# A two-model kernel whose expert weights stream from HBM: nine ring slots for eight, more expert chunks held aside and spread over the sequence, later gate-weighted selections, and a final norm on token-major rows

## The chip, the cores and the metric

One Trainium2 chip, one of its cores, one launch. The metric is the device time of the whole program in microseconds (us); lower is better. All data are float32.

## The reference, cut to what matters

The kernel runs two models one after the other on 256 tokens of 1024 features. The first has two layers (a stick-breaking attention and a dilated attention, each followed by a convolutional feed-forward net). The second has two layers (DEPTH = 2) on the 256 tokens and, in its first layer, on 256 context tokens too. Each layer modulates its input by a vector made from `c @ w_ada` (the "ada" panels), runs three branches (neighbourhood attention with a position bias, differential attention, a gated MLP), merges them, and ends in a mixture of 16 experts in which every expert picks its 32 best tokens:

```python
def ec_moe(h, w_r, w1, w3, w2):
    aff = jax.nn.softmax((h @ w_r).astype(jnp.float32), axis=-1)
    gate, idx = lax.top_k(jnp.swapaxes(aff, 1, 2), cap)          # cap = 32
    xin = jax.vmap(lambda hb, ib: hb[ib])(h, idx)
    hid = jax.nn.silu(jnp.einsum('becd,edf->becf', xin, w1)) * jnp.einsum('becd,edf->becf', xin, w3)
    ye = jnp.einsum('becf,efd->becd', hid, w2) * gate[..., None].astype(h.dtype)
    return jax.vmap(lambda yb, ib: jnp.zeros((n, D), h.dtype).at[ib.reshape(-1)].add(yb.reshape(-1, D)))(ye, idx)
```

After the last layer comes `rmsnorm(x, g_final)`. Each layer's experts have 16 x 3 matrices of 1024 x 1024, 201 MB, and each weight is used once.

## The kernel before

**Chunks.** `weight_chunks` (L196) lists all weights in the order in which TensorE needs them, cut into chunks of 1 MB (SLOT = 2048 words in each of 128 partitions). SyncE (`@block.sync`, L1205) walks the list and issues one DMA a chunk into a ring of NSLOT = 8 slots; before a chunk goes out it waits until the chunk eight places earlier has been used (L1225). TensorE waits for a chunk's semaphore and then reads it.

**Chunks held aside.** Some expert chunks don't go through the ring. `held` (L232) names them: places 8 to 15 of the expert chunks in layer 0 and places 8 to 17 in layer 1. They go to parts of SBUF that are free at the time (`held_slots`, L445), and SyncE issues them before the ring chunks named in `early`: the first 5 (7 in layer 1) once the attention is over, 3 more once the gates of the merge are done. So when the first expert starts, a stock of 8 + 8 chunks (8 + 10 in layer 1) can lie in SBUF.

**Experts** (L1149 to L1178). A layer has 192 expert chunks. Expert e takes 8 chunks for w1 and w3 (`expert_up`), then 4 for w2 of expert e-1 (`expert_down`), then a transpose of its hidden rows (`expert_turn`); the matmuls are at L1120. In layer 0 an expert has 64 rows (32 tokens and 32 of the context), in layer 1 it has 32, so that a chunk costs 8 matmuls of 512 columns in layer 0 and 16 of 256 in layer 1. Experts are handled in packs of four: `gather` (L1063, matmuls L1074) collects the tokens of a pack with a 0/1 selection matrix SEL, after e = 2, 6, 10 for the next pack; `scatter` (L1092, matmuls L1100) adds a finished pack back. `turn_gates` (L1078), after e = 1, transposes GSEL, the selection weighted by the gates, which VectorE makes (L1906) right after the first pack's copies and ahead of expert 0.

**Router.** After `w_out` TensorE makes the router's logits (L1033, L1041), VectorE and ScalarE turn them into affinities, TensorE transposes those (L1050), then does the ada panels of this place (`ada_gap`, 3 panels in layer 0 and 2 in layer 1: `ada_part`, L622, reads two chunks and frees their slots; `ada_fold`, L638, reads what ScalarE has copied from a part), and then waits for VectorE's top-k, which ends at L1860 (`pos_ready`), to transpose the places (L1059). VectorE builds SEL0 (L1883), and `gather(0)` starts.

**From layer 0 to layer 1.** After the last expert TensorE does two ada parts, `scatter(3)`, two folds; then the squares' mean (L553, L563), two more ada parts, and, once ScalarE has scaled and shifted the normed input (`scale_shift`, L2012), the first panel of w_in, two folds, the second panel.

**GpSimd's queue** issues the small loads. In each layer of the second model, once `dma_free` is set: lambda, norm and router rows, then the position bias, which is written to a scratch tensor, sheared from there into another one with 8 DMAs (L2334), and loaded as tiles with 16 DMAs (L2340). VectorE uses the tiles at L1658.

**The end.** `norm(X, S)` squares on ScalarE, sums on TensorE (L553, L563), VectorE multiplies (L1306), TensorE transposes 16 blocks (L1195), ScalarE copies, and SyncE stores the result with one DMA (L1227).

## Time and profile before

| | us |
|---|---|
| median of 3 runs (lowest to highest) | 2883.66 (2879.49 to 2886.35) |
| the profiled execution | 2883.96 |
| its span in the profile | 2882.2 |
| TensorE matmul busy | 2611.2 (91%) |
| VectorE busy | 810.2 (28%) |
| ScalarE busy | 449.5 (16%) |
| GpSimd busy | 55.4 (2%) |
| TensorE matmul, L1120 (experts) | 595.4 in 4384 instructions |
| chain that ended last: TensorE L506 (the feature-major projections) | 40% |
| chain that ended last: DMA of expert weights to the ring | 22% |

How to read it: the profile gives one execution, cut into busy time by engine and by source line; PE is TensorE, PEld its weight loads, DVE VectorE, ACT ScalarE, POOL GpSimd, SP SyncE. A "window" row gives what each engine did in a stretch, the granted TensorE clock, the busy share of the 16 DMA engines and what they moved. A timeline row gives start, duration, line, operation, what was written and read, the count, and in brackets how long the engine sat idle before and what released it. From these two the experts' stretches can be taken apart: layer 0's run from 1523 to 1993 us, layer 1's from 2415 to 2859 us.

### The profile page before, as it was taken

Reading aid. Unit: us, or ns where it says so; the run is one execution under the profiler, and the core shown is the slowest. Engines: PE = TensorE matmul, PEld = TensorE weight load, DVE = VectorE, ACT = ScalarE, POOL = GpSimd, SP = SyncE. Lnnn points to the kernel's source line nnn. Section 1 sums busy time; section 2 is a strip of 40 time slices with the busy share of each in tenths; the row PEclk is TensorE's granted clock in tenths of the full one; section 3 lists DMA queues with packets and bytes.
Section 4 is the critical chain, followed back from the end, with each engine's and each line's share of the span. In section 5 each row is a group of like instructions: output and inputs, shape, how many; then the busy total and the mean of one; then the engine's idle time right before and its main releaser. Section 6 shows DMA issues by size and latency. Waiting matters only on the chain.

```text
span 2882.2 us, 30967 instructions
## 1 busy us (share of the span) xinstructions
PE 2611.2 (91%) x13335; PEld 1547.2 (54%) x13335; DVE 810.2 (28%) x1764; ACT 449.5 (16%) x1002; POOL 55.4 (2%) x85
## 2 busy tenths in 40 slices
PE   8999999999999999999999898987999998666665
PEld 5678878578873445444444342332556885232322
DVE  2535511435512454332121121112344422010101
ACT  1320010230011022222021101112111311000001
POOL 1000000000003000000000000000200000000000
PEclk9999999999999999999999999999999999776877
DMA  8654444464456111121527999999721367999996
GB/s 276 222 162 149 173 161 146 163 217 146 169 173 168 67 59 59 44 73 59 204 105 324 420 421 421 421 421 386 178 88 67 124 262 322 421 421 421 420 421 259
DMA packets 201019, 663.81 MB, mean 230 GB/s; under 512 B 13426, under 2 KB 58784, under 8 KB 151732
## 3 DMA queue, kind: packets, MB, share of 16 engines
q1 hardware_dynamic: 192912, 641.97, 58.2%
q0 software_dynamic: 7776, 19.81, 3.1%
q8 instruction: 106, 1.74, 0.3%
q14 instruction: 29, 0.24, 0.0%
q10 hardware_dynamic: 196, 0.06, 0.0%
HBM read 660.67 MB, written 9.57 MB: 233 GB/s over the span
## 4 chain that ended last, share of the span: by engine, by line
PE 72%; DMA 23%; DVE 3%; ACT 2%; issue 1%; ACTq 0%; DVEq 0%
PE ps L506 40%; DMA ring<-in_w_e 22%; PE ps L527 8%; PE ps L1120 7%; PE ps L687 5%; PE ps L1074 1%; PE ps L622 1%; PE ps L1100 1%; PE ps L935 1%; PE ps L957 1%; PE ps L890 1%; PE ps L903 1%; DMA ring<-in_w_ada 1%; PE ps L878 1%; PE ps L553 1%
## 5 line engine op out<-in xcount | busy, mean ns | idle before, releaser
L506 PE MATMUL ps<-normed,ring 128*128 128x256 f32 (+1 forms) x3456 | 942.8, 433 | 12.4 <-ACT normed L2012 8.8
L506 PEld LDWEIGHTS ps<-normed,ring 128*128 128x128 f32 x3456 | 653.6, 191 | 279.3 <-issue 201.3
L1120 PE MATMUL ps<-ring,arena 128*32 128x256 f32 (+1 forms) x4384 | 595.4, 527 | 195.6 <-DMA ring<-in_w_e 187.3
L1120 PEld LDWEIGHTS ps<-ring,arena 128*32 128x32 f32 (+1 forms) x4384 | 194.9, 133 | 576.7 <-DMA ring<-in_w_e 286.8
L506 PE MATMUL ps<-arena,ring 128*128 128x256 f32 (+1 forms) x832 | 254.0, 462 | 1.3 <-DVE small L1248 1.3
L527 PE MATMUL ps<-ring,normed 128*128 128x512 f32 x512 | 222.8, 593 | 0.0
L506 PEld LDWEIGHTS ps<-arena,ring 128*128 128x128 f32 x832 | 156.1, 190 | 88.1 <-issue 73.1
L1329 DVE COPY arena<-ps 128x256 f32<-128x256 f32 (+1 forms) x102 | 55.9, 554 | 418.4 <-PE ps L506 173.1
L527 PEld LDWEIGHTS ps<-ring,normed 128*128 128x128 f32 x512 | 96.2, 190 | 116.2 <-issue 116.1
L687 PE MATMUL ps<-arena,ring 128*128 128x256 f32 x704 | 152.3, 379 | 0.0
L687 PEld LDWEIGHTS ps<-arena,ring 128*128 128x128 f32 x704 | 133.8, 190 | 18.2
L2268 ACT ACTIVATE normed<-ps 32x256 f32<-32x256 f32 (+1 forms) x96 | 42.8, 446 | 552.5 <-PE ps L1120 551.8
L1335 DVE TENSOR_TENSOR arena<-ps,small 128x256 f32<-128x256 f32 x128 | 51.9, 423 | 259.7 <-PE ps L506 210.8
L1920 DVE SCALAR_TENSOR_TENSOR arena<-arena,ps 128x512 f32<-128x512 f32 (+1 forms) x32 | 17.7, 554 | 375.0 <-ACT arena L2260 375.0
L1566 DVE SCALAR_TENSOR_TENSOR residual<-ps,small,residual 128x256 f32<-128x256 f32 x120 | 53.0, 481 | 197.8 <-PE ps L1100 126.4
L2089 ACT ACTIVATE arena<-arena,small 128x512 f32<-128x512 f32 (+3 forms) x64 | 43.1, 674 | 343.9 <-DVE small L1686 219.6
L1925 DVE SCALAR_TENSOR_TENSOR arena<-arena,ps 128x512 f32<-128x512 f32 (+1 forms) x32 | 17.7, 554 | 244.1 <-PE ps L1120 244.1
L2019 ACT ACTIVATE arena<-arena 128x512 f32<-128x512 f32 (+2 forms) x26 | 19.8, 762 | 380.9 <-DVE arena L1399 276.7
L2183 ACT ACTIVATE arena<-ps 128x512 f32<-128x512 f32 (+1 forms) x48 | 23.6, 491 | 281.6 <-PE ps L506 281.5
L1768 DVE SCALAR_TENSOR_TENSOR arena<-arena,ps 128x512 f32<-128x512 f32 (+1 forms) x48 | 26.6, 554 | 142.9 <-PE ps L506 142.8
L1737 DVE TENSOR_REDUCE small<-ps 128x1 f32<-128x512 f32 (+1 forms) x48 | 28.9, 602 | 105.6 <-PE ps L935 104.8
L2260 ACT ACTIVATE arena<-ps 128x512 f32<-128x512 f32 (+1 forms) x32 | 15.7, 491 | 265.0 <-PE ps L1120 265.0
(252 smaller groups left out, 1788.9 us busy)
## 6 DMA issues: line engine op xcount, KB each, us to landing
ring<-in_w_e SPq DMA_DIRECT2D x366, 1024.0 KB, 17.8
ring<-in_w_in SPq DMA_DIRECT2D x56, 1024.0 KB, 7.4
ring<-in_w_ada SPq DMA_DIRECT2D x48, 1024.0 KB, 7.4
ring<-in_ffn_w_up SPq DMA_DIRECT2D x88, 512.0 KB, 5.9
ring<-in_ffn_w_down SPq DMA_DIRECT2D x22, 1024.0 KB, 5.0
ring<-in_dil_w_qkv SPq DMA_DIRECT2D x18, 1024.0 KB, 5.1
arena<-in_w_e SPq DMA_DIRECT2D x14, 1024.0 KB, 13.2
ring<-in_sb_w_qkv SPq DMA_DIRECT2D x12, 1024.0 KB, 12.9
```

The lines of the kernel that those rows point to most:

```text
L506: ins = mm(o[:, 0:n], slots[k // 4][:, k % 4, f * P:(f + 1) * P], src[:, k, 0:n], start=k == 0, stop=k == kts - 1)
L527: ins = mm(o, src[:, k, t * P:(t + 1) * P], slots[k // 4][:, k % 4, :], start=k == 0, stop=k == KT - 1)
L553: ins = mm(o[32 * (k % 4):32 * (k % 4) + 32, 0:n], mean[:, 0:32], src[:, k, 0:n], start=k < 4, stop=k >= 4)
L622: ins = mm(o[32 * (k % 4):32 * (k % 4) + 32, :], silu_pad[:, k, :], slots[k // 4][:, k % 4, :], start=k < 4, stop=k >= 4)
L687: ins = mm(outs[f][:, 0:S], slot[:, k, f * P:(f + 1) * P], HID[:, 2 * j + k, :], start=j == 0 and k == 0, stop=j == FT // 2 - 1 and k == 1)
L1120: ins = mm(o[w * g:w * g + w, 0:cols], lhs(2 * c + j), slot[:, j, g * cols:(g + 1) * cols], start=c == 0 and j == 0, stop=c == KT // 2 - 1 ...
L1329: ve.tensor_copy(dst, o[:, 0:n]).then_inc(banks.freed["v"], banks.free("v"))
L1335: ve.tensor_tensor(dst, o[:, 0:S], rstd[:, 0:S], ALU.mult).then_inc(banks.freed["v"], banks.free("v"))
L1566: ins = ve.scalar_tensor_tensor(X[:, f, t], o[:, t], gt[:, f, s:s + 1], X[:, f, t], ALU.mult, ALU.add)
L1737: ve.tensor_reduce(nmax[:, n % 2, c:c + 1], o[:, k0:2 * S], AX.X, ALU.max, negate=True).then_inc(v_step.sem, v_step.up())
L2089: return se.activation(s, s if src is None else src, ACT.Exp, bias=nmax[:, n % 2, k:k + 1], scale=scale, accum_out=ssum[:, n % 2, k:k + 1])
L2268: ins = se.activation(YE[q][r:r + CAP, (e - 1) // 4, g * cols:(g + 1) * cols], o[g * w + q * CAP:g * w + (q + 1) * CAP, 0:cols], ACT.Copy)
```

## The change

- `NSLOT` goes from 8 to 9. The 2048 words for it come from the constants (one table dropped; `suffix`, `sb_keep`, `sb_neg`, needed in the first model alone, go to the arena by a load of their own) and from `dynamic_dma_scratch_size`, the memory for GpSimd's DMA descriptors, which goes from 8192 to 4096.
- The held chunks: 9 in layer 0 (one more, loaded once w_out is done), 12 in layer 1 (one more in the residual of the context, one more once w_out is done). In layer 0 they are no longer consecutive but at places 8, 13, 18, 22, 27, 31, 36, 40 and 45; in layer 1 at 8 to 19.
- The gate-weighted selection is made anew after expert 3 and transposed after expert 4. In layer 1 a pack's input has its own, narrower shape (`XINS`).
- The ada panels: 2 of the 4 between the layers stand behind w_in's first panel now, and the other 2 are used after the scatter. At the router all but one part come before the affinities' transpose, and all but one fold of layer 0 (both of layer 1) after the transpose of the places.
- The final norm works on token-major rows: transposes of X, ScalarE's squares with a row sum, VectorE's multiply by the root and by a gain row that GpSimd loads during the last experts (`FINAL_GAIN`), two stores.
- The shears of both layers' position bias are done in the first model, into a scratch tensor each; the tile loads wait until VectorE has copied the gated MLP's input (`tile_turn`). Large GpSimd DMAs are cut in three.

```diff
-NSLOT = 8
+NSLOT = 9
-ASIDE_FIRST, ASIDE_THEN = (5, 7), 3
+ASIDE_FIRST, ASIDE_THEN, ASIDE_LAST = (5, 8), 3, 1
+ASIDE_AT = ((8, 45, 22, 40, 27, 36, 13, 31, 18), (8, 9, 10, 11, 12, 13, 14, 15, 16, 17, 18, 19))
...
             panel(w, c0 * BRANCH)
+            if i and c0 == 6:
+                ada_panels(ADA_LAYER // 2)
...
-        held = [len(out) + NSLOT + j for j in range(ASIDE_FIRST[i] + ASIDE_THEN)]
+        held = [len(out) + at for at in ASIDE_AT[i]]
...
+        early[len(out) + NSLOT - 2 * ADA_ROUTER[i]] = held[then:]
...
         if i == 0:
-            ada_panels(ADA_LAYER)
+            ada_panels(ADA_LAYER // 2)
...
-        held_slots = [held_first[:ASIDE_FIRST[i]] + held_then for i in range(DEPTH)]
+        held_slots = [held_first + held_then + [view(2048, SLOT)],
+                      held_first + [view(2048, SLOT), view(6144, SLOT), X[:, :, S:2 * S]] + held_then
+                      + [view(1024, 2, 8192)[:, :, 0:1024]]]
...
                 if last:
                     ada_part()
                     ada_part()
+                    ada_fold()
+                    ada_fold()
                 gemm_T(1, H, qtok, fresh=True)
+                if last:
+                    ada_part()
+                    ada_part()
+                gemm_N(1, H, qtiles)
                 if last:
                     ada_fold()
                     ada_fold()
-                gemm_N(1, H, qtiles)
...
+                for _ in range(ADA_ROUTER[i] - 1):
+                    ada_part()
                 pe.wait_ge(aff_ready.sem, aff_ready.nth("pe"))
...
-                ada_gap(ADA_ROUTER[i])
+                for _ in range(ADA_ROUTER[i] - 2):
+                    ada_fold()
+                ada_part()
                 pe.wait_ge(pos_ready.sem, pos_ready.nth("pe"))
...
+                ada_fold()
+                ada_fold()
                 pe.wait_ge(P_ready.sem, P_ready.nth("pe"))
...
-                    if e == 1:
+                    if e == 4:
                         turn_gates()
+                    if e == 2:
+                        pe.wait_ge(P_ready.sem, P_ready.nth("pe"))
...
-                if not last:
-                    ada_part()
-                    ada_part()
                 scatter(3)
-                if not last:
-                    ada_fold()
-                    ada_fold()
...
-            mean_square(H, S)
...
+            for half in range(2):
+                pe.wait_ge(banks.freed["v"], scattered[4 * half - KT + 3])
+                for t in range(ST):
+                    o = banks.open("a", "v")
+                    pe.wait_ge(*banks.due)
                     for f in range(4):
-                        ins = nc.tensor.transpose(o[:, f * P:(f + 1) * P], H[:, 4 * half + f, t * P:(t + 1) * P], ident)
+                        ins = nc.tensor.transpose(o[:, f * P:(f + 1) * P], X[:, 4 * half + f, t * P:(t + 1) * P], ident)
...
+            for t in range(ST):
+                sp.wait_ge(final_ready.sem, 2 * t + 2)
+                sp.dma_start(out[0, t * P:(t + 1) * P, :], OUTT[:, t, :]).then_inc(loads["out"], 16)
...
(VectorE, the final norm)
+            for t in range(ST):
+                for half in range(2):
+                    d = slice(half * 512, (half + 1) * 512)
+                    ve.scalar_tensor_tensor(OUTT[:, t, d], turned[t, half], RCOL[:, t:t + 1], FINAL_GAIN[:, d], ALU.mult, ALU.mult
+                                            ).then_inc(final_ready.sem, final_ready.up())
...
(ScalarE, the transition and the final norm)
                 norm(X, 2 * S)
+                if last:
+                    ada_copies(ADA_LAYER // 2)
                 scale_shift(i, 0, 2)
...
+                    ins = se.activation(OUTT[:, t, half * 512:(half + 1) * 512], o, ACT.Square, accum_out=SSQ[:, t, half:half + 1])
...
(GpSimd)
+                gp.wait_ge(tile_turn.sem, tile_turn.nth("gp"))
                 for hh in range(2):
...
+            gp.wait_ge(dma_free.sem, dma_free.nth("gp"))
+            gp.dma_start(FINAL_GAIN, dram(a["g_final_2"], 0, [[0, P], [1, D]])).then_inc(loads["final_gain"], 16)
...
-    nc = bacc.Bacc("TRN2", target_bir_lowering=False, num_devices=1, dynamic_dma_scratch_size=8192)
+    nc = bacc.Bacc("TRN2", target_bir_lowering=False, num_devices=1, dynamic_dma_scratch_size=4096)
```

## Rows read from the trace of the kernel before

**Rows 1.** Page, part 2: GB/s moved in 40 equal slices of the span.
```profile
GB/s 276 222 162 149 173 161 146 163 217 146 169 173 168 67 59 59 44 73 59 204 105 324 420 421 421 421 421 386 178 88 67 124 262 322 421 421 421 420 421 259
```

**Rows 2.** L1120 alone by window: span, PE, PEld, clock, DMA share, GB/s.
```profile
1611.70:1969.50 357.80, 266.82 (x1144) 74.94 (x1144) 1.00 1.01 421
...
2433.50:2850.00 416.50, 240.19 (x2688) 89.03 (x2688) 0.76 1.01 420
```

**Rows 3.** Windows of 5 us, layer 0's first experts: engines, clock, DMA share, GB/s.
```profile
1520.00:1525.00 5.00, 3.54 (x25) 2.21 (x26) 4.48 (x10) 0.00 (x0) 0.00 (x0) 1.00 0.05 20
...
1545.00:1550.00 5.00, 5.00 (x26) 1.72 (x24) 0.69 (x1) 0.60 (x1) 0.00 (x0) 1.00 0.37 156
1550.00:1555.00 5.00, 5.00 (x27) 1.58 (x23) 0.69 (x1) 0.00 (x0) 0.00 (x0) 1.00 0.00 0
```

**Rows 4.** Timeline, layer 0's router to its first expert.
```profile
1506.46 0.28 DVE L1860 TENSOR_SCALAR arena<-arena 32x256 f32<-32x256 f32 x1
...
1510.10 0.30 PE L1059 MATMUL ps<-constants,arena 32*128 32x32 f32 x2
...
1512.42 9.33 PE L1074 MATMUL ps<-arena 128*128 128x128 f32 x64 [2.02 <-DVE arena L1883]
...
1523.22 13.95 PE L1120 MATMUL ps<-ring,arena 128*64 128x512 f32 x64 [1.46 <-DVE arena L1899]
```

**Rows 5.** Timeline, end of layer 0's experts and start of layer 1.
```profile
1974.60 8.60 PE L1120 MATMUL ps<-ring,arena 128*64 128x512 f32 x32 [2.43 <-ACT arena L2274]
...
1985.05 0.59 ACT L2268 ACTIVATE arena<-ps 32x512 f32<-32x512 f32 x1
...
1990.38 2.74 PE L622 MATMUL ps<-ring,small 128*32 128x512 f32 x16 [3.50 <-issue]
...
1993.05 1.22 PE L1100 MATMUL ps<-arena,normed 128*128 128x256 f32 x2
...
2008.81 3.64 PE L622 MATMUL ps<-ring,small 128*32 128x512 f32 x32
...
2011.63 7.97 ACT L2012 ACTIVATE normed<-normed,small 128x256 f32<-128x256 f32 x16 [1.36 <-DVE normed L1554]
```

**Rows 6.** Timeline: layer 1's router to its first expert.
```profile
2405.80 0.28 DVE L1860 TENSOR_SCALAR arena<-arena 16x256 f32<-16x256 f32 x1
...
2407.45 0.29 PE L1059 MATMUL ps<-constants,arena 16*128 16x16 f32 x2
...
2414.58 7.11 PE L1120 MATMUL ps<-ring,arena 128*32 128x256 f32 x128 [1.46 <-DVE arena L1899]
```

**Rows 7.** Timeline: layer 0's row sums, then the end of the program.
```profile
1495.00 0.60 ACT L2215 ACTIVATE arena<-ps 128x512 f32<-128x512 f32 x1
...
1496.63 0.23 DVE L1818 TENSOR_TENSOR small<-ps,small 128x64 f32<-128x64 f32 x1 [0.67 <-ACT small L2240]
...
2861.81 2.69 DVE L1566 SCALAR_TENSOR_TENSOR residual<-ps,small,residual 128x256 f32<-128x256 f32 x6 [0.37 <-PE ps L1100]
...
2873.22 3.65 PE L1195 MATMUL ps<-constants,normed 128*128 128x128 f32 x16 [4.57 <-DVE normed L1306]
...
2877.76 0.40 SPq L1227 DMA_DIRECT2D out<-arena  x1
```

**Rows 8.** Page, part 6: DMA issues, count, KB each, us to landing.
```profile
out<-arena SPq DMA_DIRECT2D x1, 1024.0 KB, 4.0
...
constants<-in_const_table SPq DMA_DIRECT2D x1, 192.0 KB, 2.6
```

**Rows 9.** Timeline of the tile loads and their use; DMAs of the shear tensor to landing.
```profile
2045.70 0.81 POOL L2334 DMA_DIRECT2D na_bias_shear<-na_bias_scratch  x1 [21.24 <-issue]
2051.38 10.38 POOL L2340 DMA_DIRECT2D arena<-na_bias_shear  x16 [4.87 <-DMA na_bias_shear<-na_bias_scratch]
...
2116.42 3.35 DVE L1658 TENSOR_TENSOR arena<-arena,constants 128x3072 f32<-128x3072 f32 x1
...
DMA to landing us min/median/max: 2.7/7.2/21.6
```

More of the change, by code:

```diff
@@ L329, in build @@
         chunk_used = sem("chunk_used")
-        loads = {n: sem(f"load_{n}") for n in ("ident", "consts", "gain_rows", "rows", "x", "ctx", "bucket", "router", "out", "relb", "gm",
-                                               "lam", "bias_out", "bias_shear", "bias_in", "rpb_out", "rpb_shear", "rpb_in")}
+        loads = {n: sem(f"load_{n}") for n in ("ident", "consts", "sb_tables", "gain_rows", "rows", "x", "ctx", "bucket", "router", "out", "relb", "gm",
+                                               "lam", "bias_out", "bias_shear", "bias_in", "rpb_out", "rpb_shear", "rpb_in", "final_gain")}
         load_count = {n: 0 for n in loads}
@@ L704, in _ @@
             pe.wait_ge(loads["consts"], 16)
+            pe.wait_ge(loads["sb_tables"], 16)
             pe.wait_ge(sc_ready.sem, sc_ready.nth("pe"))
```

167 lines of the change are left out of this document (100 added, 67 removed).

## The prediction

> **What bounds the kernel now.** I read the page's slices first [rows 1]. The DMA engines run flat at about 421 GB/s in two stretches of about seven slices each, and nowhere else: these are the experts of the second model's two layers. Next the experts' matmuls by window [rows 2]: in layer 0 TensorE is busy 267 of 358 us while the DMA share is 1.01, in layer 1 240 of 417. So both stretches last as long as the bytes do, and a chunk of 1.049 MB costs 1.049/421 = 2.49 us. A chunk that is already in SBUF when the first expert starts takes 2.49 us off the stretch, if the engines would have been idle while it was fetched; so does any idle time of theirs that goes. TensorE's speed doesn't matter there: in layer 1 its granted clock is 0.76 of full, between its levels of 1.2 and 2.4 GHz, at the same 420 GB/s [rows 2]. Outside these stretches no wait of TensorE for the ring is in the list of waits, so a deeper ring gains nothing there.
>
> One place inside the first stretch is not bound by DMA: windows of 5 us show 156 and 0 GB/s from 1545 to 1555 [rows 3]. The eight held chunks are consecutive, so TensorE frees no slot while it uses them, the ring fills up, and SyncE has nowhere to load to.
>
> The Trainium skill ("DMA: Bandwidth & Descriptors", Specifications) gives a limit of about 358 GB/s from HBM for one core. The trace shows 420 and 421 for hundreds of microseconds [rows 2], so the measurement decides. By that page a chunk would be 2.93 us, and the five chunks below would be worth 14.6 us instead of 12.5.
>
> **Part 1, layer 0's experts: 15.5 us less.** Three terms.
> (a) *Earlier start.* Top-k is ready at 1506.46 + 0.28 = 1506.74, but TensorE is in the ada panels and turns the places only at 1510.10 [rows 4]. With all but one part moved ahead, into the wait for the affinities, and two folds behind, the turn can come at 1506.8: 3.3 us earlier. The selection takes what it did (1510.10 to 1512.42, 2.3 us), and the two folds, about 1.9 us, fit inside. Late next is VectorE's selection, as before.
> (b) *Stock.* 9 + 9 chunks for 8 + 8: 2 x 2.49 = 5.0 us. They can be fetched in time: from 1520 to 1525 the engines moved 20 GB/s [rows 3], ring full.
> (c) *Idle time.* The two windows lose 5 x (1 - 156/421) + 5 = 8.2 us. With the held chunks at every fourth or fifth place TensorE frees a slot nearly all the time. The danger is the pause of a gather. Up to the first, TensorE uses 32 chunks, 26 of them in the ring, in about 59 us (14.0, then twice 20.8, and turns); DMA loads 57/2.49 = 23 meanwhile. It is three chunks in arrears, 7.5 us, about as long as a gather. So nearly nothing is lost; I leave 1 us for it and take 7.2. Bounds: 4 (half stays idle) to 10 (the windows beside these, too).
>
> Making the gate-weighted selection twice over costs VectorE four operations after expert 3, each of the size of L1906 (about 1.2 us), while it is busy 28% of the span and TensorE waits for DMA: nothing, and 5 us once if that cover were gone.
>
> **Part 2, from layer 0 to layer 1: 3.0 us less.** Expert 15's w2 takes TensorE until 1983.2 and the copies until 1985.64, but `scatter(3)` starts at 1993.05 [rows 5]: between them are two ada parts whose chunks come behind the last experts' in the stream. That wait of 7.4 us goes. It is partly given back. The parts after the squares' mean (2008.81 to 2012.45) are now copied by ScalarE ahead of `scale_shift`, which began at 2011.63: it starts at about 2013.1, 1.5 us later [rows 5]. And two ada parts now stand in TensorE's full stretch behind w_in's first panel: 2.7 to 3.6 us by the two rows of L622; I take 2.9. The folds weigh the same: one pair has moved into the gap. Sum 7.4 - 1.5 - 2.9 = 3.0; bounds 1 and 5. The chunks these parts need are the fourteen behind the last expert; by then the stream has had 30 us, enough for twelve, and slots are freed in time.
>
> **Part 3, layer 1's experts: 7.0 us less.** The stock is 9 + 12 for 8 + 10: 3 x 2.49 = 7.5 us. Top-k is ready at 2406.08 and the places are turned at 2407.45 [rows 6]; that becomes 2406.1, of which the folds, now between the turn and the gather, take back half: 0.7 us. Between the end of w_out at 2392.9 and the first freed slot at about 2415 the stream has seven chunks to fetch, 17.4 us, so they fit, with 4 to 5 us to spare. Against that GpSimd loads the gain row into 128 partitions during the last experts, 0.5 MB: 1.2 us of a full stream. 7.5 + 0.7 - 1.2 = 7.0; bounds 5 (one chunk's fetch comes too late) and 9.
>
> **Part 4, the end: 6.7 us less.** The last scatter's addition ends at 2861.81 + 2.69 = 2864.50, the store is issued at 2877.76, and lands 4.0 us later, at 2881.8 [rows 7, 8]. In the new order TensorE needs 16 transposes at 0.228 us (L1195: 3.65 for 16), of which those of the first half start at about 2864.0, when the scatter's matmuls are done: the last is through at 2867.6. ScalarE's last square starts then; from the start of such a square to the root in VectorE's hands the router needs 1496.63 - 1495.00 = 1.63 us [rows 7]: 2869.3. Four multiplies of 128 x 512 from PSUM, 0.69 each like L1925: the second half of the result is ready at 2872.0. Its store is 512 KB; 192 KB took 2.6 us and 1024 KB 4.0 [rows 8], so 3.1: 2875.1. Gain 6.7; bounds 4.5 (a store as long as a full one, slower transposes) and 8.
>
> The Trainium skill ("DMA: Bandwidth & Descriptors", Anatomy of one DMA) puts a DMA at about 2.0 us plus its bytes at 436 GB/s. That would be 3.2 us for the half store, and 4.4 for the whole, where the row shows 4.0.
>
> **Part 5, the first model and the small loads: nothing.** The shears move from the start of each second-model layer into the first feed-forward net, where DMA moves 150 to 220 GB/s [rows 1] and TensorE needs a chunk only every 6.5 us with nine in stock; if that cover failed, the price is the 35 us in which one layer's shears and w_in share the engines, in part. `sb_tables` is needed 25 us after it is issued. The tile loads wait for a copy at 931.9 and 2047.4 instead of for the shears (903 and 2051): for VectorE's use at 1014.8 and 2116.4 there are 83 and 69 us [rows 9].
>
> **The sum.** 15.5 + 3.0 + 7.0 + 6.7 = 32.2 us off the profiled execution's 2883.96: 2851.8. The median of the runs, 2883.66, is 0.3 lower, so I predict 2851.5. Low end: 10 + 3.3 + 5.0, 5, 9, 8 sum to 40, and 2843; high end: 4 + 2 + 5, 1, 5, 4.5 sum to 21.5, and 2862.
>
> **The rivals.**
> *Rival A, the ring still fills.* If TensorE's pauses (gathers, turns) stop the stream as much as the consecutive chunks did, (c) gives nothing, and what the exchange saves is shorter by 7.2 us; if the ada parts in layer 1 wait for their chunks as well, part 2 gives nothing: 2851.5 + 7.2 + 3.0 = 2862. For it: a gather is as long as the arrears. Against: after layer 0's first four experts the engines never paused before. Chance 12%.
> *Rival B, the load only moves.* If the engines have no idle time before the first experts to take the extra chunks, the stock (5.0 and 7.5 us) is paid for before: 2864. Against: 20 GB/s from 1520 to 1525 [rows 3]. Chance 4%.
> *Rival C, slower: half the descriptor memory makes the position tiles late.* With the present memory GpSimd got seven shears out and then stood 21.2 us before the eighth [rows 9]. Sixteen tile loads went out in 10.4 us. If the halved memory lets a few be in flight, say four, at 7.2 us each to landing they need 29 us, and there are 69: no loss. If it lets only one, they need 16 x 7.2 = 115 us: 46 us late in layer 1 and 32 in layer 0, since VectorE stands at L1658 and the attention behind it. That is 78 - 32 = 46 us slower, 2930. It decides from 4.3 us a load on in layer 1 (69/16), and makes the kernel slower from about 7 us a load. Chance 4%.
> *Rival D, better still.* The windows beside the idle ones go too, and the store is short: 2843. It lies within the forecast's range.
>
> **Chances.** Forecast with D 80%, A 12%, B 4%, C 4%. The range, 2841 to 2864, holds the forecast's own 2843 to 2862, and A and B's centres. A measurement of this kernel can tell about 0.2%, 5.8 us, from no change. Faster by more: 0.94 (the forecast, A and B nearly whole). Within: 0.02. Slower: 0.04, which is C.
>
> **What would show each step.** (a) L1059 in layer 0 comes within 0.2 us of L1860's end, and the first L1120 13 us after that, as now. (b, c) No window of 5 us between the first experts and the last at under 400 GB/s, but for the first release; L1120's last ring wait in layer 0 about 12 us sooner after the first expert's start. Part 2: `scatter(3)` starts with the last copy, and L2012 begins 1.5 us later after the root than now. Part 3: the stretch from the first L1120 to the last is 6 us shorter. Part 4: from the last L1566 to the last issue of SyncE 7.5 us instead of 13.3. Part 5: L1658's successor starts right behind the copy before it in both layers. The prediction is wrong if TensorE waits for the ring outside the experts, if ada parts wait, or if L1658 is released by a DMA.

## The result, and the profile after

The changed kernel's median is 2852.36 us (2851.24 to 2854.49), and 2883.46 us for the kernel before, measured beside it: a ratio of 0.9897, interval 0.9885 to 0.991. The forecast was 2851.5, in a range from 2841 to 2864. The total came within 1 us; the parts did not. Two were larger than forecast, three smaller. One of the four executions of a later kernel, r1_router_back, took 3221.39 us at a granted clock of 0.80 over the whole span; its median below, 2855.95, has it in it (2855.75 without), its ratio does not.

Both programs can be cut at the same events, and the stretches of the two profiled executions compared. A stretch runs from the start of one event to the start of the next, and in the last two rows to or from the end of the last expert matmul. "w2" is the group of 32 matmuls that ends a layer's experts. "Router" is a layer's router matmul, "turn" the four transposes of the gated MLP's weights, behind w_in's first two panels in layer 1 (L850 before, L869 after).

| stretch | before, us | after, us | change | forecast |
|---|---|---|---|---|
| start to layer 0's router | 1489.99 | 1489.02 | -1.0 | 0 |
| router to first expert, layer 0 | 33.23 | 32.22 | -1.0 | -3.3 |
| first expert to expert 15's w2 | 451.38 | 436.38 | -15.0 | -12.2 |
| w2 to the turn | 71.91 | 71.70 | -0.2 | -3.0 |
| turn to layer 1's router | 346.35 | 346.39 | 0.0 | 0 |
| router to first expert, layer 1 | 21.72 | 23.72 | +2.0 | -0.7 |
| first to last expert matmul, layer 1 | 442.61 | 436.47 | -6.1 | -6.3 |
| last expert matmul to the span's end | 25.01 | 15.00 | -10.0 | -6.7 |
| span | 2882.2 | 2850.9 | -31.3 | -32.2 |

The page of the changed kernel, the same line as [rows 1]. The two plateaus are there at the same height, and the last slice holds more, since the end is shorter:

```profile
GB/s 300 218 196 167 164 169 129 163 230 159 155 159 138 111 59 30 74 56 78 150 122 350 415 421 421 421 421 393 197 69 79 119 227 339 421 421 421 420 421 315
```

Windows of 5 us in layer 0's experts, after, as [rows 3]: us, busy time of PE, PEld, DVE, ACT, POOL, granted clock, DMA share, GB/s. Where 156 and 0 GB/s stood, the stream is full. One dip is left, at 1590:

```profile
1545.00:1550.00 5.00, 5.00 (x26) 1.59 (x24) 0.11 (x1) 0.00 (x0) 0.00 (x0) 1.00 1.01 419
1550.00:1555.00 5.00, 5.00 (x26) 1.72 (x24) 0.69 (x1) 0.00 (x0) 0.00 (x0) 1.00 1.02 424
...
1585.00:1590.00 5.00, 5.00 (x33) 2.99 (x33) 2.73 (x8) 0.00 (x0) 0.00 (x0) 1.00 0.99 410
1590.00:1595.00 5.00, 5.00 (x26) 1.72 (x24) 0.18 (x1) 0.60 (x1) 0.00 (x0) 1.00 0.96 331
```

The timeline of layer 0's router after, as [rows 4]. The places are turned at 1505.62, right behind top-k (1505.56), as forecast, 16.6 us after the router's matmul instead of 20.1; but the two folds take 3.62 us instead of 1.9 and the gather 10.38 instead of 9.33:

```profile
1505.62 0.42 PE L1083 MATMUL ps<-constants,arena 32*128 32x32 f32 x2 [2.20 <-DVE arena L1891]
1505.97 3.62 PE L651 MATMUL ps<-constants,arena 128*128 128x32 f32 x16
...
1509.40 10.38 PE L1100 MATMUL ps<-arena 128*128 128x128 f32 x64
...
1521.24 1.94 PE L1150 MATMUL ps<-ring,arena 128*64 128x512 f32 x8 [1.46 <-DVE arena L1931]
```

Windows of 1 us of the same place show what went with it. TensorE was busy 16% and 61% of two of them, waiting for ScalarE; at about 1501.6 the granted clock fell from its level of 2.4 GHz to that of 1.2, in the middle of a part, and rose again only at 1515.2:

```profile
1498.00:1499.00 1.00, 0.16 (x2) 0.11 (x2) 0.75 (x5) 0.97 (x4) 0.00 (x0) 1.00 1.00 336
1499.00:1500.00 1.00, 0.61 (x6) 0.38 (x4) 0.69 (x2) 1.00 (x3) 0.00 (x0) 1.00 1.07 442
...
1501.00:1502.00 1.00, 1.00 (x12) 0.29 (x8) 0.93 (x4) 0.00 (x0) 0.00 (x0) 0.78 0.96 401
1502.00:1503.00 1.00, 1.00 (x8) 0.00 (x0) 0.93 (x4) 0.00 (x0) 0.00 (x0) 0.50 0.95 401
...
1515.00:1516.00 1.00, 1.00 (x10) 1.00 (x10) 0.00 (x0) 0.00 (x0) 0.00 (x0) 0.90 0.00 0
```

So it was low for 13.6 us. Before, by the same kind of windows, it was low twice at this place, from 1499.8 to 1503.2 and from 1513.5 to 1516.9, 6.8 us together.

The way from layer 0's experts to layer 1, as [rows 5]. The scatter starts 2.5 us behind expert 15's w2; the squares' mean starts at 1979.90 in place of 2003.20. Then come parts and folds twice, at 1985.51 and at 2010.21:

```profile
1957.62 8.78 PE L1150 MATMUL ps<-ring,arena 128*64 128x512 f32 x32 [2.43 <-ACT arena L2332]
1968.89 0.97 PE L1127 MATMUL ps<-arena,normed 128*128 128x256 f32 x2 [2.48 <-ACT arena L2326]
...
1985.51 3.64 PE L635 MATMUL ps<-ring,small 128*32 128x512 f32 x32
1989.08 1.97 PE L651 MATMUL ps<-constants,arena 128*128 128x32 f32 x16
...
1993.80 16.48 PE L519 MATMUL ps<-normed,ring 128*128 128x256 f32 x60 [0.77 <-ACT normed L2068]
2010.21 3.64 PE L635 MATMUL ps<-ring,small 128*32 128x512 f32 x32
```

Layer 1's router, as [rows 6]: the turn comes after 4.52 us without work, and the clock falls right behind its start, at 2389.0; folds 3.62 us, gather 5.54 (4.04 before). The first line is that of the kernel before:

```profile
2409.08 4.04 PE L1074 MATMUL ps<-arena 128*128 128x128 f32 x32 [1.33 <-DVE arena L1883]
...
2388.76 0.29 PE L1083 MATMUL ps<-constants,arena 16*128 16x16 f32 x2 [4.52 <-DVE arena L1891]
2388.99 3.62 PE L651 MATMUL ps<-constants,arena 128*128 128x32 f32 x16
2392.42 5.54 PE L1100 MATMUL ps<-arena 128*128 128x128 f32 x32
```

And the end, as [rows 7]. The last addition ends at 2841.80, and the span 9.1 us later; before it was 2864.50 and 17.7 us:

```profile
2837.55 3.72 PE L1127 MATMUL ps<-arena,normed 128*128 128x256 f32 x16 [1.65 <-ACT normed L2326]
2838.29 3.51 DVE L1594 SCALAR_TENSOR_TENSOR residual<-ps,small,residual 128x256 f32<-128x256 f32 x8 [23.09 <-PE ps L1127]
...
2841.11 1.91 PE L1218 MATMUL ps<-constants,residual 128*128 128x128 f32 x16
...
2843.47 0.60 ACT L2346 ACTIVATE arena<-ps 128x512 f32<-128x512 f32 x1
...
2845.13 2.73 DVE L1994 SCALAR_TENSOR_TENSOR arena<-ps,small,arena 128x512 f32<-128x512 f32 x4 [0.70 <-ACT small L2351]
2846.56 1.66 SPq L1255 DMA_DIRECT2D out<-arena  x2
```

### The profile page after: what moved, and what is told of

The parts are those of the page before. It is cut to its first block, busy times and chain, and to the rows that moved or that the text cites. A ratio compares the mean times of both kernels' runs of the same rounds, so it can differ in the third digit from the quotient of the medians.

```text
span 2850.9 us, 30941 instructions
## 1 busy us (share of the span) xinstructions
PE 2604.5 (91%) x13317; PEld 1551.7 (54%) x13317; DVE 811.9 (28%) x1768; ACT 445.9 (16%) x1000; POOL 60.7 (2%) x91
## 4 chain that ended last, share of the span: by engine, by line
PE 74%; DMA 20%; DVE 3%; ACT 2%; issue 1%; ACTq 0%; DVEq 0%
PE ps L519 41%; DMA ring<-in_w_e 20%; PE ps L1150 8%; PE ps L540 8%; PE ps L700 5%; PE ps L1127 1%; PE ps L1100 1%; PE ps L635 1%; PE ps L954 1%; PE ps L976 1%; PE ps L909 1%; PE ps L922 1%; PE ps L897 1%; PE ps L651 1%; PE ps L566 0%
## 5 line engine op out<-in xcount | busy, mean ns | idle before, releaser
L1150 PE MATMUL ps<-ring,arena 128*32 128x256 f32 (+1 forms) x4344 | 588.6, 527 | 180.6 <-DMA ring<-in_w_e 172.5
L1961 DVE SCALAR_TENSOR_TENSOR arena<-arena,ps 128x512 f32<-128x512 f32 (+1 forms) x32 | 17.7, 554 | 367.6 <-ACT arena L2318 367.6
L1966 DVE SCALAR_TENSOR_TENSOR arena<-arena,ps 128x512 f32<-128x512 f32 (+1 forms) x32 | 17.7, 554 | 234.4 <-PE ps L1150 234.4
## 6 DMA issues: line engine op xcount, KB each, us to landing
arena<-in_w_e SPq DMA_DIRECT2D x16, 1024.0 KB, 10.2
```

Source lines behind the costliest of these rows:

```text
L1150: ins = mm(o[w * g:w * g + w, 0:cols], lhs(2 * c + j), part, start=c == 0 and j == 0, stop=c == KT // 2 - 1 and j == 1)
```

## The experiments

The theories at this point: the stock and the spread of the held chunks gained what the bytes say; the way to the first experts lost its gain to TensorE's low clock; the exit gave its gain back in parts and folds; the end gained more than its chain, or had luck. One table for all runs, with the stretches as above (R router, E first expert, D expert 15's w2, T turn, in us), so that each run tests its own part and is a control for the others:

| kernel | median | ratio to before, interval | R0-E0 | E0-D | D-T | R1-E1 | E1-last | end |
|---|---|---|---|---|---|---|---|---|
| before | 2883.5 | 1 | 33.23 | 451.38 | 71.91 | 21.72 | 442.61 | 25.01 |
| after | 2852.36 | 0.9897, 0.9885 to 0.991 | 32.22 | 436.38 | 71.70 | 23.72 | 436.47 | 15.00 |
| r1_router_back | 2855.95 | 0.9904, 0.9888 to 0.9921 | 33.34 | 436.24 | 71.68 | 22.37 | 436.59 | 16.63 |
| r2_warm | 2850.59 | 0.9889, 0.9872 to 0.9905 | 28.19 | 436.79 | 69.62 | 20.58 | 437.98 | 16.72 |
| r3_folds_late | 2850.35 | 0.9888, 0.9873 to 0.9903 | 30.12 | 436.23 | 70.42 | 22.81 | 436.41 | 16.52 |
| r4_exit_back | 2856.24 | 0.9908, 0.9893 to 0.9922 | 31.01 | 436.67 | 71.96 | 24.46 | 436.48 | 18.13 |
| r5_consecutive | 2862.82 | 0.9934, 0.9921 to 0.9946 | 31.04 | 446.97 | 69.94 | 23.72 | 436.56 | 15.02 |
| r6_stock_back | 2863.21 | 0.9934, 0.9921 to 0.9946 | 31.04 | 440.79 | 69.59 | 23.67 | 443.91 | 15.09 |
| r7_exit_early_parts | 2851.8 | 0.9895, 0.9882 to 0.9909 | 30.83 | 436.46 | 70.85 | 24.88 | 436.43 | 16.73 |
| r8_all_three | 2851.09 | 0.9889, 0.9874 to 0.9904 | 29.89 | 436.39 | 69.59 | 21.89 | 437.49 | 17.38 |
| r9_tail_back | 2859.43 | 0.9923, 0.9911 to 0.9936 | 30.90 | 436.49 | 69.87 | 23.71 | 435.21 | 25.26 |
| r10_after_again | 2852.20 | 0.9894, 0.9879 to 0.9909 | 32.17 | 437.32 | 70.57 | 23.72 | 436.49 | 15.06 |

The two columns of the experts, in which the DMA engines are busy nearly throughout, repeat where the code is the same: E1-last between 436.41 and 436.59 (r2 and r8 apart, which reach it sooner), E0-D between 436.23 and 436.79, with one 437.32. R0-E0, D-T and the end move by 1 to 3 us in kernels whose code there is the same. The kernel before was measured again beside each batch of runs, and the ratios are to these medians: 2883.38 us beside r1 to r4, 2882.13 beside r5 to r8, 2883.29 beside r9 and r10.

**r5_consecutive: the nine held chunks of layer 0 side by side.**

```diff
-ASIDE_AT = ((8, 45, 22, 40, 27, 36, 13, 31, 18),
+ASIDE_AT = ((8, 9, 10, 11, 12, 13, 14, 15, 16),
```

> The changed kernel with layer 0's nine held chunks consecutive again, at places 8 to 16; ring, stock and all else as in the changed kernel. The prediction's term (c) counts 7.2 us for the spread (bounds 4 to 10): 2859.5, the stretch from the first expert matmul to expert 15's w2 growing from 436.4 to 443.6 us, with one or two windows of 5 us at under 200 GB/s some 25 to 35 us after the first expert. The traces leave 15.0 us for stock and spread together, of which the stock's part is 5.0, so 10 us and 446.4 us would be the spread's part: 2862. Rival A (the ring fills anyway, and the shorter stretch is due to the stock and the earlier gates): no change, 2852.4, 436.4 us.

E0-D is 446.97, 10.6 us over 436.38, and the median 10.5 over after's. Its windows have the hole again:

```profile
1545.00:1550.00 5.00, 5.00 (x26) 1.68 (x24) 0.00 (x0) 0.00 (x0) 0.00 (x0) 1.00 0.02 8
1550.00:1555.00 5.00, 5.00 (x26) 1.72 (x24) 0.69 (x1) 0.00 (x0) 0.00 (x0) 1.00 0.16 21
1555.00:1560.00 5.00, 5.00 (x26) 1.82 (x24) 0.00 (x0) 2.76 (x5) 0.00 (x0) 1.00 0.89 329
```

Against 421 these windows lose 4.9 + 4.7 + 1.1 us, and 0.3 the one ahead of them (398): 11.0. The spread kernel loses 0.1 + 1.1 at 1585 and 1590. The difference, 9.8, is nearly the 10.6. The one dip of the spread kernel follows the first gather inside the experts, 58 us after the first expert, where the prediction had looked for such a pause and left 1 us for it:

```profile
1579.42 7.70 PE L1100 MATMUL ps<-arena 128*128 128x128 f32 x64
```

So the spread is the largest single gain of the change, and rival A (the ring fills all the same) is refuted.

**r6_stock_back: eight held chunks and eight slots, as before, but spread** (ten held in layer 1).

```diff
-NSLOT = 9
+NSLOT = 8
-ASIDE_FIRST, ASIDE_THEN, ASIDE_LAST = (5, 8), 3, 1
+ASIDE_FIRST, ASIDE_THEN, ASIDE_LAST = (5, 7), 3, 0
```

> The changed kernel with 8 ring slots, 8 held chunks in layer 0 (still spread, at 8, 45, 22, 40, 27, 36, 13, 31) and 10 in layer 1: the stock of the kernel before. Prediction: 2 x 2.49 = 5.0 us in layer 0 and 3 x 2.49 = 7.5 us in layer 1 are lost, 2865; the stretches of expert matmuls grow from 436.4 to 441.4 us (first expert matmul to expert 15's w2, layer 0) and from 436.5 to 444.0 us (first to last, layer 1). Rival B (the load only moves): the stretches grow as much, but the first experts start sooner by what is not fetched ahead, and the time stays at 2852 to 2855. Third: with a shallower ring and spread places the ring's arrears at the gathers turn into idle time, so that layer 0 loses more than 5 us, up to 9.

E1-last is 443.91 for 436.48: 7.4 us for three chunks, 2.48 each. E0-D is 440.79 for 436.38: 4.4 us for two, where 5.0 was the price. In this kernel the windows from 1585 and 1590 move 419 and 421 GB/s, so the dip of 1.2 us belongs to the larger stock; it more than covers the missing 0.6:

```profile
1590.00:1595.00 5.00, 5.00 (x26) 1.73 (x24) 0.69 (x1) 0.60 (x1) 0.00 (x0) 1.00 1.02 421
```

By rival B (the load only moves) the first experts would have started sooner here by what isn't fetched ahead, and the median stayed at 2852 to 2855. It is 2863.21; R1-E1 is 23.67 as in after (23.72), and R0-E0, 31.04, lies where r4, r5, r7 and r9 have it with after's stock (30.83 to 31.04). Rival B is refuted.

**r2_warm: TensorE kept busy in the two waits before the turn**, by 6 and 16 transposes of the identity in layer 0, 12 and 34 in layer 1, whose result is overwritten.

```diff
-                pe.wait_ge(pos_ready.sem, pos_ready.nth("pe"))
...
+                for _ in range((16, 34)[i]):
+                    nc.tensor.transpose(o[:, 0:P], ident, ident)
+                pe.wait_ge(pos_ready.sem, pos_ready.nth("pe"))
```

> The changed kernel with dummy transposes of the identity (6 and 16 in layer 0, 12 and 34 in layer 1) on TensorE in the waits for the affinities and for the places, written into the bank that is overwritten next; nothing else moves. Clock theory: the granted clock stays at 1.0 through folds and gather, the two folds take 2.0 us instead of 3.6, the first gather 9.3 or less instead of 10.4 in layer 0 and 4.0 instead of 5.5 in layer 1, so the first experts start 2.5 to 3 us sooner in each layer: 5 to 6 us faster than the changed kernel, about 2847. Rival: the folds are slow because they wait for ScalarE's copies or for their banks, and the gather because of its operands; then the dummies change nothing, 2852, or cost up to 1 us where they run over the wait.

```profile
1503.50 1.97 PE L1084 MATMUL ps<-constants 128*128 128x128 f32 x16
...
1506.86 1.97 PE L651 MATMUL ps<-constants,arena 128*128 128x32 f32 x16
...
1508.96 7.80 PE L1104 MATMUL ps<-arena 128*128 128x128 f32 x64
...
1518.22 5.37 PE L1154 MATMUL ps<-ring,arena 128*64 128x512 f32 x24 [1.46 <-DVE arena L1935]
```

The clock is 1.00 in every window from 1496 to 1522, the folds take 1.97 us, the gather starts 2.3 us after the turn, as in the kernel before, and takes 7.80. R0-E0 is 28.19, 4.0 less than after and 5.0 less than before; R1-E1 is 20.58, 3.1 less than after. With nothing changed but dummy work, that is the clock's price, and more than the 2.5 to 3 us a layer that were expected. But the median is only 1.6 to 1.8 below after's two, not 5 to 6, and the intervals overlap widely. Part of it is given back in layer 1, where E1-last is 437.98, 1.5 us more. The stock is full there 1.6 us before the first expert (4.7 in after), so it isn't short; 0.8 of the 1.5 us lie in the 5 us from 2395.6, 4 us behind the first expert, which move 351 GB/s, where after has 424 at the same distance. In this profile the stages that nobody touched took 2.7 us (start and end) and gave 2.1 (D-T); it is the quickest of its four executions, and after's is the second slowest of four.

**r3_folds_late: the two folds behind the gather.**

```diff
                 ins.then_inc(banks.filled, 1)
-                ada_fold()
-                ada_fold()
                 pe.wait_ge(P_ready.sem, P_ready.nth("pe"))
...
                 gather(0)
+                ada_fold()
+                ada_fold()
```

> The changed kernel with the two folds behind the first gather instead of ahead of it, on TensorE and on VectorE. If the folds hold the gather back (selection ready at 1508.0 and gather at 1509.4 in layer 0; 2390.3 and 2392.4 in layer 1), the gather starts 1.4 and 2.1 us sooner; the folds' 3.6 us at the low clock (2 us at the high one) then stand ahead of the first expert only where VectorE's pack copies don't cover them (1.5 us of wait there now). Net per layer between 1.4 us sooner and 1 us later; total 0 to 3.5 us faster than the changed kernel, 2849 to 2852. If only the clock matters: no change.

R0-E0 is 30.12, 2.1 less than after, and R1-E1 22.81, 0.9 less. The gather starts 2.02 us behind the turn's end in place of 3.4, and the folds stand at full clock in the gap before the first expert, which they make 0.2 us longer (1.6 us for 1.46). The clock is low from 1501.4 to 1511.6, 3.4 us less than in after (gather 9.45 us).

**r1_router_back: the parts and folds around the turn as before.**

```diff
-                for _ in range(ADA_ROUTER[i] - 1):
-                    ada_part()
                 pe.wait_ge(aff_ready.sem, aff_ready.nth("pe"))
...
-                for _ in range(ADA_ROUTER[i] - 2):
-                    ada_fold()
-                ada_part()
+                ada_gap(ADA_ROUTER[i])
                 pe.wait_ge(pos_ready.sem, pos_ready.nth("pe"))
...
-                ada_fold()
-                ada_fold()
```

> The changed kernel with the router's ada panels where they were before: all parts and folds between the affinities' transpose and the places' transpose. The prediction's step (a) says that this loses what the move brought, 3.3 us in layer 0 and 0.7 in layer 1, so 4 us slower than the changed kernel (about 2856). The theory after the traces: the move left TensorE idle for 2 to 4.5 us ahead of the places, the granted clock fell to 0.50, and folds and gather got slower, so that the first expert of layer 0 came only 1.0 us sooner after the router's matmul (33.2 to 32.2 us) and that of layer 1 2.0 us later (21.7 to 23.7 us). By it this kernel is 1.0 us slower in layer 0 and 2.0 us faster in layer 1: 1 us faster than the changed kernel, 2851.4, and from the router's matmul (L1053) to the first expert matmul (L1150) it shows 33.2 and 21.7 us again. A third possibility: slots are freed 3 to 5 us later, the stock of 18 and 21 chunks isn't full at the first expert, and up to 5 us are lost on top.

R0-E0 33.34 and R1-E1 22.37, within 0.7 us of before's in both. With the new order the profiles of after, r4 to r7, r9 and r10 show 30.83 to 32.22 and 23.67 to 24.88. So the order gained 1.1 to 2.5 us in layer 0 and lost 1.3 to 2.5 in layer 1: together, nothing. The experts' stretches are after's within 0.15 us, so the third possibility, a stock that isn't full, is out. The median is 3.4 to 3.6 us over after's, near the 4 us that step (a) of the prediction asks for, but 1.7 of this profile's 3.1 lie ahead of layer 0's router and 1.6 in the end, where the code is the same, so it isn't evidence for the order.

**r4_exit_back: the old order from layer 0's last expert to layer 1**, with the order of the loads that belongs to it.

```diff
                     ada_part()
                     ada_part()
-                    ada_fold()
-                    ada_fold()
                 gemm_T(1, H, qtok, fresh=True)
-                if last:
-                    ada_part()
-                    ada_part()
-                gemm_N(1, H, qtiles)
                 if last:
                     ada_fold()
                     ada_fold()
+                gemm_N(1, H, qtiles)
...
+                if not last:
+                    ada_part()
+                    ada_part()
                 scatter(3)
+                if not last:
+                    ada_fold()
+                    ada_fold()
```

> The changed kernel with the four ada panels between the layers where they were before, in the chunk list and on the engines: two parts ahead of the last scatter, two behind the squares' mean, no copies ahead of scale and shift. The prediction's part 2 says that the move brought 3.0 us: this kernel would be at 2855. The traces put the move at 0.2 us, since what the scatter gains (6.3 us) is given back by the copies ahead of scale and shift (1.4), by a lower clock in the first panel (1.0) and by two parts in TensorE's full stretch (3.6): 2852.5. If the move costs more than it brings, below 2851.

D-T is 71.96, as before (71.91). The new order has eight profiles: 69.59 to 71.70, mean 70.42. The change gained 1.5 us there on average, with 0.2 in its own profile and 1.3 in the repeat. The median, 2856.24, is 3.9 over after's, more than the prediction's 3.0 asks for, but this profile's start is 2.4 us longer than after's and its end 3.1, both with the same code.

**r7_exit_early_parts: the scatter first, then the two parts that stand behind w_in's first panel, ahead of the squares' mean**, so that TensorE has nothing between the panels.

```diff
                 scatter(3)
+                if not last:
+                    ada_part()
+                    ada_part()
...
                 gemm_T(1, H, qtok, fresh=True)
-                if last:
-                    ada_part()
-                    ada_part()
                 gemm_N(1, H, qtiles)
```

> The changed kernel with all four ada panels between the layers directly behind the last expert in the chunk list again, but used as follows: last scatter, two parts (copied by ScalarE between its squares and the sum), squares' mean, two folds, two parts (copied behind scale and shift, as in the kernel before), first panel and second panel of w_in without a part in between, two folds. Theory from the traces: the 3.6 us of the two parts in the full stretch and the 1.4 us of the copies ahead of scale and shift go, 1.1 us of copies ahead of the sum come: from the start of expert 15's w2 to the end of the second panel 72.3 us now, 68.4 then; 4 us faster, 2848.5. Rival: the parts' chunks and w_in's first panel come too late in the stream (ten chunks behind the last expert instead of six), and TensorE waits for the panel up to 10 us less what it gains: 2852 to 2858.

D-T is 70.85, inside the range of the order before it (69.59 to 71.70): nothing. The 3.6 us of the parts between the panels are gone, and this stands in their place:

```profile
1986.49 1.92 PE L633 MATMUL ps<-ring,small 128*32 128x512 f32 x16 [0.58 <-issue]
1995.52 16.37 PE L517 MATMUL ps<-normed,ring 128*128 128x256 f32 x64 [7.11 <-issue]
```

With all of the parts' chunks ahead of them in the stream, w_in's first chunks come too late, and TensorE stands 7.11 us: in the trace the second of them has landed at 1995.4, 0.1 us before the panel starts. In this order the stream, not TensorE, limits the exit, as the rival expected.

**r9_tail_back: the old final norm and one store; no gain row.**

```diff
-                for t in range(ST):
-                    o = banks.open("a", "v")
...
-                        ins = nc.tensor.transpose(o[:, f * P:(f + 1) * P], X[:, 4 * half + f, t * P:(t + 1) * P], ident)
+                        ins = nc.tensor.transpose(o[:, f * P:(f + 1) * P], H[:, 4 * half + f, t * P:(t + 1) * P], ident)
...
+            pre_norm(X, g_final)
...
-            gp.dma_start(FINAL_GAIN, dram(a["g_final_2"], 0, [[0, P], [1, D]])).then_inc(loads["final_gain"], 16)
```

> The old end alone: norm of the whole second half first, then the turns, one store; no gain row is loaded. By the prediction's sum part 4 was worth 6.7 us and the gain row cost 1.2: from the last expert matmul to the span's end 15.0 + 6.7 = 21.7 us, from the first to the last expert matmul of layer 1 436.47 - 1.2 = 435.3, and the time 2852.4 + 5.5 = 2857.9. By the traces before and after it was worth 10.0 us: end 25.0 us, time 2852.4 + 10.0 - 1.2 = 2861.2. A third reading: the after trace's end (15.0) was short because its clock was full there; the other runs' 16.5 to 16.7 is typical, part 4 is worth 8.4, and the end of this kernel is 24 to 26 us, whichever way its clock falls. If GpSimd's load costs nothing, the stretch stays at 436.4.

```profile
2833.89 5.38 PE L1127 MATMUL ps<-arena,normed 128*128 128x256 f32 x16 [1.65 <-ACT normed L2313]
...
2837.58 2.21 DVE L1596 SCALAR_TENSOR_TENSOR residual<-ps,small,residual 128x256 f32<-128x256 f32 x5 [0.24 <-PE ps L1127]
...
2848.51 3.65 PE L1221 MATMUL ps<-constants,normed 128*128 128x128 f32 x16 [4.58 <-DVE normed L1336]
...
2853.05 0.40 SPq L1257 DMA_DIRECT2D out<-arena  x1
```

The end is 25.26 us, of which 17.7 lie behind the last addition (2839.79); with the new end that part is 9.1 to 9.2 in all ten profiles. So the new chain is worth 8.5 us in each of them. The rest of the end, from the last expert matmul to the last addition, is 5.9 us where the clock was full in the scatter (3.72 us of matmuls: after, r5, r6, r10) and more where it wasn't: 5.42 us of matmuls in r2, 6.78 in r4. E1-last is 435.21 for 436.47: GpSimd's gain row costs 1.26 us of the stream, as forecast. The third reading (8.4 us, an end of 24 to 26) came nearest; the median, 2859.43, lies between the first two.

**r10_after_again: the changed kernel, nothing edited.**

> The changed kernel once more, nothing edited: a control. If the spread of the stages that DMA doesn't bind is chance in the clock, the two expert stretches repeat (436.4 and 436.5 within 0.3 us), while the way from layer 0's last expert to layer 1's router moves between 416.0 and 418.3 and the end between 15.0 and 18.1. If the end of 15.0 us belongs to this kernel, it comes again within 0.3.

The two expert stretches are 437.32 and 436.49, the first 0.9 longer, outside the 0.3 that I allowed; the same dip is deeper (375 and 315 GB/s at 1585 and 1590, 1.8 us for 1.2). D-T is 70.57 for 71.70: the scatter's first eight matmuls, at low clock in after (1.06 us a pair), ran at full clock here (0.59). The end is 15.06, again within 0.3. With the same code at the end, after, r5, r6 and r10 show 15.00 to 15.09, and r1 to r4, r7 and r8 16.52 to 18.13, by the clock that the scatter gets. Since four of ten profiles have the short end, two of them of this kernel don't show whether it belongs to the kernel or to chance.

**r8_all_three: r2's transposes, r3's order and r7's exit together.**

> The changed kernel with the dummy transposes of the earlier run, the folds behind the first gather, and the ada parts between the layers as in the run beside it. If the three add up: the dummies took 4.0 and 3.1 us off the way from the router's matmul to the first expert, the later folds 2.1 and 0.9 us; both act on the same wait, so together at most 5 and 4 us; with 4 us from the transition 12 us less than the changed kernel at most, 2841. If the experts' stream, not the first expert's start, decides from there on (the ring isn't full yet when the first expert begins), the earlier start in layer 1 brings no more than 3 us: 2843 to 2846. If the dummies' clock gain doesn't last into the experts, 2848.

R0-E0 29.89, R1-E1 21.89, D-T 69.59, but the end 17.38 and E1-last 437.49. The median, 2851.09, is above all three that I had expected, and no gain over r2 or r3. The ways to the first experts are 1.7 and 1.3 us longer than in r2, with the same transposes. With the folds behind the gather TensorE has nothing to do for 2.02 us between turn and gather, and the clock, which r2 held, fell from 1510.5 to 1513.9 (gather 9.33 us for 7.80) and in layer 1 from 2387.7 to 2391.1. A timeline row and a window of layer 0:

```profile
1509.10 9.33 PE L1097 MATMUL ps<-arena 128*128 128x128 f32 x64 [2.02 <-DVE arena L1916]
...
1510.00:1515.00 5.00, 5.00 (x32) 5.00 (x32) 2.44 (x6) 0.00 (x0) 0.00 (x0) 0.66 0.90 374
```

Against after's profile the start, layer 1's experts and the end took 1.2, 1.0 and 2.4 of the 6.3 us that the three stages gained. No version was measured that beats after by more than the intervals.

## Why the prediction was right or wrong

**The total was right in part by luck: errors cancelled.** By the table, the ways to the first experts gained 2.3 and 2.7 us less than forecast, the exit 2.8 less and layer 1's experts 0.2 less: 8.0 us. Layer 0's experts gained 2.8 more, the end 3.3 and the time ahead of layer 0's router 1.0 more: 7.1 us. The sum, 31.3, is 0.9 below the 32.2 forecast.

*Part 1 (a), 3.3 us forecast, 1.0 in after's profile (2.4 at most in the others).* The step that the turn follows top-k at once was right (1505.62 after 1505.56; after the router's matmul it came 3.5 us sooner). The step that failed is "the two folds, about 1.9 us, fit inside": they took 3.62, the gather started 3.78 us after the turn instead of 2.32, and took 1.05 more than before. The sum priced the moved work at durations of full clock, and the clock was low for 13.6 us instead of 6.8. r2 has the turn at the same distance from the router matmul (16.6 us in both), the folds inside and the clock full, and reaches the first expert 4.0 us sooner. That the fall came from TensorE's thinner work just ahead is what r2 speaks for; what makes the clock fall was not measured apart. The sign that the prediction set for this step, the first expert 13 us after the turn, came out as 15.6.

*(b), 5.0 forecast, 4.4 measured (r6).* Right, less half of the dip of 1.2 us, which r6 doesn't have.

*(c), 7.2 forecast, 10.6 measured.* The mechanism was right; the term was mis-sized. The sum counted two windows [rows 3], 8.2 us, and left out their neighbours: before, the window from 1555 moved 328 GB/s and that from 1565 338, another 2.1 us:

```profile
1555.00:1560.00 5.00, 5.00 (x27) 1.90 (x24) 0.00 (x0) 0.50 (x1) 0.00 (x0) 1.00 0.91 328
...
1565.00:1570.00 5.00, 5.00 (x26) 1.59 (x24) 0.43 (x1) 0.60 (x1) 0.00 (x0) 1.00 0.90 338
```

That is 10.2 us of the 10.6 between the kernel before and r6, both with eight slots and eight held chunks (451.38 and 440.79). Between r5 and after, with nine of each, it is 11.0 less the dip's 1.2, 9.8 of the 10.6. The other 0.4 and 0.8 I can't place. The bound of 10 named the neighbours, and what was measured lies beyond it; the central value should have held them.

*Part 2, 3.0 forecast, 1.5 on average.* The wait of 7.4 us did go, as forecast. Given back were 1.4 us ahead of the first panel (1.5 forecast: from the end of the squares' sum, L576, to the panel 6.3 us for 5.0), 3.6 for the two parts between the panels (2.9 forecast: I had taken the row at the lower end, [rows 5] had 3.64), and a term that the sum lacked: the first panel itself, 18.1 to 18.5 us in the new order for 17.3 in before and in r4, where its matmuls took 0.275 us each (16.48 for 60), against 0.221 in the old order's last 52. The granted clock was 0.50 from 1993.1 to 1999.9 in after, and full there in the old order. The row of the kernel before:

```profile
2019.66 11.49 PE L506 MATMUL ps<-normed,ring 128*128 128x256 f32 x52 [0.83 <-ACT normed L2012]
```

In after the scatter, too, took longer, 8.85 us for 7.99, by the clock that it got; in r10, at full clock, it took 7.2.

*Part 3, 7.0 forecast, 4.1 measured.* The stock (7.4 for 7.5) and the gain row (1.26 for 1.2) were right. The term of +0.7 for the earlier turn was -2.0, by the same failed step as in (a): the turn came 1.5 us sooner, but after 4.52 us without work the clock was low for the folds and the start of the gather; the gather started 3.7 us after the turn instead of 1.6, and took 1.5 more. r2, at full clock, is 3.1 us quicker.

*Part 4, 6.7 forecast, 10.0 measured.* Squares to VectorE (1.66 us for 1.63), multiplies (2.73 for 2.76) and the half store (3.0 at most, from the end of the last multiply, for 3.1) were right. By the Trainium skill ("DMA: Bandwidth & Descriptors", Anatomy of one DMA) the half store would be an estimated 3.2 us, and the trace agrees within 0.2; the page fits its formula to DMAs that GpSimd issues, and this store is SyncE's. The mis-sized term is the transposes: the row they were priced by, 3.65 us for 16 [rows 7], was measured at a granted clock of 0.50, after VectorE's norm; right behind the scatter they run at full clock, 1.91 us, and begin 0.7 us before the last addition's end. That is 1.9 us. The other 1.4 came with the scatter, which ran at full clock in this profile and at half clock for part of it in the kernel before; that is luck. Over the ten profiles with this end the mean is 16.2 us, 8.9 less than in the two with the old one (25.01 and 25.26).

*Part 5, nothing forecast, nothing found.* GpSimd now gets three shears out and then stands, four such waits of 7.5 to 13.8 us, all before 232 us. Of the tile loads ten go out at once and six after a wait:

```profile
178.96 2.42 POOL L2390 DMA_DIRECT2D na_bias_shear<-na_bias_scratch  x3 [10.11 <-issue]
...
945.27 3.95 POOL L2406 DMA_DIRECT2D arena<-na_bias_shear  x6 [6.50 <-issue]
...
2042.39 3.94 POOL L2406 DMA_DIRECT2D arena<-na_bias_shear  x6 [6.81 <-issue]
...
2099.27 3.35 DVE L1689 TENSOR_TENSOR arena<-arena,constants 128x3072 f32<-128x3072 f32 x1
```

In layer 1 they are all issued by 2046.3, 53 us ahead of their use at L1689, and none takes more than 8.2 us to land, so rival C is refuted. Its own arithmetic had a slip: with 16 loads of t us each in the two layers the loss is 32 t - 152 us, which passes the gain of 32 us at 5.8 us a load, not at 7. That case, loads one after the other, didn't come: ten were issued before the first wait. The 1.0 us ahead of layer 0's router isn't the change's: with the same code there, that router comes at 1488.9 to 1491.4 in the runs.

**What stays open.** Why the clock falls in one profile and not in another with the same code at that place: the last scatter ran at full clock in four of ten. No run kept TensorE busy at the exit or at the end, so the clock's part there is read from the traces and was not tested by an edit of its own. The medians of r2, r3, r7 and r8 differ from after's by 0.6 to 2.0 us, less than the end alone moves between profiles, so none of these orders is shown to be better than the change.

## What to carry to other kernels

Price DMA-bound stretches by bytes, chunk by chunk, and count every window under the plateau, the half-empty ones too: here the stock of layer 1 and the gain row came out within 0.1 us of that price, and the spread of layer 0 within 0.8. When work is moved ahead of a wait of TensorE, price what follows the wait at both levels of the clock, from rows at either: here the folds at half clock (3.62 us) and the slower gathers (1.05 and 1.5 us more) make up what the two routers missed, while the last scatter, after the same wait of 1.65 us in each profile, ran at either level. A chunk that stands before another in the one stream delays it: an order that suits TensorE can move its wait instead of removing it, as r7 did.

## What the runs showed of the hardware

- The granted clock can fall in the middle of full work. TensorE was busy 16% and 61% of the two microseconds from 1498 and fully from 1500; at 1501.6 the clock went to 0.50, and stayed there until 1515.2, through an idle time of 2.20 us and 9 us of folds and gather. In layer 1 it fell at 2389.0, behind 4.52 us without work, until 2395.8.
- The level is worth a factor of 1.8 to 1.9 on matmuls with a weight load each and at most 256 columns: two folds 1.97 us and 3.62, 16 transposes 1.91 and 3.65, a scatter's 16 matmuls 3.72 and up to 6.78.
- With 6 to 34 transposes of 128 x 128 in two waits the clock stayed at 1.00 up to the first expert (r2). With the same transposes, but the two folds gone from between turn and gather, it fell to 0.50 in the gather, for 3.4 us in each layer (r8).
- One core's 16 DMA engines held 421 GB/s for 350 us at a time in every run, and a broadcast load by GpSimd of 0.5 MB took 1.26 us of that; its bytes at 421 would take 1.25.
